# A two-layer transformer kernel in split fp32: the SBUF start addresses of the low weight halves, of the matmul operands and of the last product's operand are shifted

## The reference, cut to what matters

```
D_MODEL = 2048; SEQ = 256; DEPTH = 2; D_FF = 5632
for i in range(DEPTH):
    a = _rmsnorm(h, norm_mix[i])
    y = _mla(a, ...) if i == 0 else _swa_sinks(a, ...)
    h = h + y
    h = h + _conv_ffn(_rmsnorm(h, norm_ffn[i]), ffn_w_in[i], ffn_conv_w[i], ffn_conv_b[i], ffn_w_out[i])
return _rmsnorm(h, final_norm)
```

## Time and profile before

| | |
|---|---|
| median of 3 runs | 1988.99 us (1988.56 to 1989.11) |
| the profiled execution: its own time | 1988.18 us |
| its span, first to last instruction | 1986.3 us |
| TensorE busy | 1974.7 us, 99% of the span |
| DVE, ACT, POOL busy | 71%, 50%, 7% |
| granted TensorE clock, mean | 0.999 of full |
| moved by DMA | 379.69 MB, mean 191 GB/s |

### The profile page before, as it was taken

One profiled execution on the slowest core, in us unless ns is written; L12 is line 12 of the kernel. 1 busy time (PEld: TensorE's weight loads), 2 busy tenths in 40 slices (PEclk: granted clock), 3 DMA queues, 4 the chain that ended last, 5 costly groups with the idle time before them and its releaser, 6 DMA issues.

```text
span 1986.3 us, 33224 instructions
## 1 busy us (share of the span) xinstructions
PE 1974.7 (99%) x11726; PEld 1746.8 (88%) x11726; DVE 1418.6 (71%) x1969; ACT 991.5 (50%) x1180; POOL 143.8 (7%) x157
## 2 busy tenths in 40 slices
PE   9999999999999999999999999999999999999998
PEld 8998888888888888888899999888888888888886
DVE  6856788877887787554567668778877887765444
ACT  6556445555545554334446654555455555544443
POOL 1112220000000000110120004100000000011000
PEclk9999999999999999999999999999999999999999
DMA  8566655555555555556565435655555555576664
GB/s 300 178 195 162 195 188 190 180 194 197 183 176 191 193 197 192 190 181 201 191 229 190 136 129 173 199 191 189 172 195 194 190 188 187 197 251 214 216 193 140
DMA packets 106871, 379.69 MB, mean 191 GB/s; under 512 B 12107, under 2 KB 12684, under 8 KB 106668
## 3 DMA queue, kind: packets, MB, share of 16 engines
q1 hardware_dynamic: 102332, 362.22, 55.4%
q0 software_dynamic: 4176, 16.07, 3.2%
q10 hardware_dynamic: 288, 0.33, 0.1%
HBM read 368.09 MB, written 10.49 MB: 191 GB/s over the span
## 4 chain that ended last, share of the span: by engine, by line
PE 96%; DVE 2%; DMA 1%; ACT 0%; issue 0%; SPq 0%; ACTq 0%
PE ps L429 46%; PE ps L432 24%; PE ps L822 4%; PE ps L821 4%; PE ps L823 4%; PE ps L723 2%; PE ps L724 2%; PE ps L725 2%; DMA raw<-weights 1%; DVE w_lo L1172 1%; PE ps L761 1%; PE ps L784 1%; PE ps L459 1%; PE ps L460 1%; PE ps L458 1%; PE ps L772 1%
## 5 line engine op out<-in xcount | busy, mean ns | idle before, releaser
L1172 DVE TENSOR_TENSOR w_lo<-raw,w_hi 128x1024 fp32r<-128x1024 f32 (+1 forms) x678 | 824.8, 1230 | 493.5 <-ACT w_hi L861 472.3
L861 ACT ACTIVATE w_hi<-raw 128x1024 fp32r<-128x1024 f32 (+1 forms) x678 | 710.2, 1054 | 773.3 <-PE ps L432 455.1
L429 PE MATMUL ps<-op_in,w_hi 128*128 128x512 f32 x2992 | 1026.5, 391 | 0.4 <-DVE w_lo L1172 0.4
L432 PE MATMUL ps<-op_in,w_lo 128*128 128x256 f32 x2992 | 812.4, 282 | 0.0
L429 PEld LDWEIGHTS ps<-op_in,w_hi 128*128 128x128 f32 x2992 | 549.0, 188 | 104.5 <-issue 0.7
L432 PEld LDWEIGHTS ps<-op_in,w_lo 128*128 128x128 f32 x2992 | 565.1, 189 | 15.7
L429 PE MATMUL ps<-op_ffn,w_hi 128*128 128x512 f32 x704 | 243.1, 390 | 0.0
L432 PE MATMUL ps<-op_ffn,w_lo 128*128 128x256 f32 x704 | 195.9, 282 | 0.0
L429 PEld LDWEIGHTS ps<-op_ffn,w_hi 128*128 128x128 f32 x704 | 131.1, 188 | 26.5
L822 PE MATMUL ps<-w_lo,op_ffn 128*128 128x512 f32 x352 | 138.7, 394 | 0.0
L821 PE MATMUL ps<-w_hi,op_ffn 128*128 128x512 f32 x352 | 138.0, 392 | 0.0
(11 more groups left out here) (218 smaller groups left out, 2054.2 us busy)
## 6 DMA issues: line engine op xcount, KB each, us to landing
raw<-weights SPq DMA_DIRECT2D x662, 512.0 KB, 4.0
raw<-weights SPq DMA_DIRECT2D x16, 384.0 KB, 3.3
bias_rows<-brow POOLq DMA_DIRECT2D x1, 6144.0 KB, 36.2
win_bias<-bias_rows POOLq DMA_DIRECT2D x4, 1024.0 KB, 8.1
h<-xt SPq DMA_DIRECT2D x8, 256.0 KB, 6.7
raw<-weights SPq DMA_DIRECT2D x8, 256.0 KB, 5.7
x_tok<-x_rows SPq DMA_DIRECT2D x4, 512.0 KB, 8.9
h_rows<-h_blocks POOLq DMA_DIRECT2D x16, 128.0 KB, 5.7
```

The source lines that it names most:

```text
L429: return mm(ps[:, bank, 0:2 * T], whi, op, start=start, stop=stop)
L432: return mm(ps[:, bank, 0:T], wlo, op[:, 0, :], start=False, stop=False)
L861: f(w_hi[s][:, 0:cols], raw[s][:, 0:cols], ACT.Copy).then_inc(hi_ready, 1)
L1172: v.tensor_tensor(w_lo[s][:, 0:cols], raw[s][:, 0:cols], w_hi[s][:, 0:cols].bitcast(F32), ALU.subtract).then_inc(lo_ready, 1)
```

## The change

No instruction is added, removed or moved: the program of every engine is the same, with the same waits, and only the addresses of tiles differ. A helper `at_256(place)` moves the next free byte up to one whose remainder by 256 is `place`. It is called ahead of `w_hi`, where it moves nothing, ahead of `w_lo`, and ahead of the operands. The offset of `op_ffn[1]` against `op_ffn[0]` grows from 160 to 192 bytes, and `par` loses 256 bytes that nothing used.

```
@@ -184,7 +184,13 @@
     raw = [new(f"raw{s}", [P, CH]) for s in range(SLOTS)]
+    def at_256(place):
+
+        top[0] += (place - top[0]) % 256
+
+    at_256(128)
     w_hi = [new(f"w_hi{s}", [P, CH], F32R) for s in range(SLOTS)]
+    at_256(64)
     w_lo = [new(f"w_lo{s}", [P, CH], F32R) for s in range(SLOTS)]
     h = new("h", [P, KT, T])
...
-    par = new("par", [P, 7 * P])
+    par = new("par", [P, PC_END])
...
-    top[0] = (top[0] + 127) // 128 * 128 + 32
+    at_256(64)
     ra = region(KT * 2 * T * 4)
     op_in = place("op_in", [P, KT, 2, T], F32R, ra)
...
-    rg = region(FT * 2 * T * 4 + 160)
+    rg = region(FT * 2 * T * 4 + 192)
     r_o = rg + 57344
-    op_ffn = [place("op_ffn0", [P, FT, 2, T], F32R, rg), place("op_ffn1", [P, FT, 2, T], F32R, rg + 160)]
+    op_ffn = [place("op_ffn0", [P, FT, 2, T], F32R, rg), place("op_ffn1", [P, FT, 2, T], F32R, rg + 192)]
```

## The result

The changed kernel takes 2006.32 us in the median (2006.23 to 2006.98, 4 runs) against 1988.78 us before in the same comparison: a ratio of 1.0089, 95% interval 1.0072 to 1.0107. It is 17.5 us slower. The prediction was 1980.9 us, within 1967 to 1997.

What follows compares the result with a forecast made beforehand. TensorE's matmul periods were taken to bound the kernel. Gains of 4.1 (512 columns), 3.4 (256 columns) and 0.6 us (token triples) sum to 8.1; 1988.18 less that gives 1980.1, plus 0.8 for the median 1980.9 us, range 1967 to 1997.

Steps and rivals of the forecast that it cites:

- What bounds the kernel: Whole kernel: how fast TensorE's matmuls follow each other sets the time, neither HBM nor the splits; TensorE busy 1974.7 of 1986.3 us.
- I take the 1.0 ns as the price of the moving tile's odd start: 512-column matmuls in pairs: 230.0 ns against the last product's 229.0, the difference put down to a start off multiples of 64.
- differ in exactly that: The three groups with the most matmuls: claimed to differ in whether moving or loaded tiles start at multiples of 64.
- 512 columns in pairs: The 512-column half of each pair (512 and 256 columns together): 4144 x 1.0 ns, 4.1 us gained.
- 256 columns: Pairs and narrow triples, 5584 matmuls of 256 columns: 0.6 of the 1.0 ns each, 3.4 us gained.
- Token triples: 288 matmuls at 118.3 ns with the loaded tile at 160: 2.1 ns less each, 0.6 us gained.
- the bound "nothing": 512-column matmuls in pairs: lower bound of the gain, since mixing two lengths could cost that nanosecond as well.
- Last product at nothing: 1056 matmuls with starts at multiples of 64 before and after: costed at nothing; one nanosecond would be 1.1 us.
- The slower rival: Loads of `w_lo` from the operand's start by 256 clash with streaming: 1.5 ns a load, 6.9 us, 1996 us; chance 0.18.
- The large gain: All matmuls: the 5% surplus a column is two reads meeting, removable by good placement; 1894 us at its far end; chance 0.07.
- The argument from the Trainium skill: TensorE's array: two independent ports, so loading takes no bandwidth from the running matmul; the sum would be 0, 1989 us.
- The 8 and 13 ns over N/2.4 + 2.5: Periods of 116.8 (256 columns) and 229.0 ns (512) against 109.2 and 215.8: something costs more than the page allows.

Runs made afterwards that it cites:

- first map: Kernel without the model: uniform rows and pairs at 64 placements of streamed and loaded tile; 226.7 to 234.4 ns per 512-column matmul, pairs 349.9 ns at the changed kernel's distances.
- second map: The first map's kernel with other rows (smaller loads, 384 columns, 16-byte steps, triples, pairs); at the changed kernel's distances, last product 686.7 ns a triple, pairs 340.0 ns.

## Why the prediction was wrong

- **What bounds the kernel** was right. (The shares read with it hold for the two long stretches of the earlier trace rows only: between 1045 and 1203 us DVE is at 69% and ACT at 57%, and ACT's 42% is that of the last product. Nothing rests on this.) Periods of matmuls set the time, and three of them account for the whole difference of 18.1 us. DVE, ACT and the DMAs took no part, and the early, paced part kept its time.
- **The step that failed** is "I take the 1.0 ns as the price of the moving tile's odd start", and with it the sentence that the groups "differ in exactly that". The groups differed in distance and in sequence too, and I picked the remainder of the start by 64. Moving every matmul tile by 32 bytes changed nothing (346.8, 228.9 and 116.7 ns again), so that remainder has no price. What sets the period is the distances between loaded and streamed tiles, here (-32, -32) in pairs and -64 in the last product, together with what runs ahead of a row. Not even a distance has a price of its own: the changed kernel's (+64, 0) gave 350.0 ns and, behind another order, 340.0.
- **512 columns in pairs**: expected -4.1 us. **256 columns**, in pairs and narrow triples: expected -3.4 us. Measured: pairs, both halves together, +13.8 us, narrow triples +1.0 us. **Token triples**: expected 2.1 ns less each, measured, over the eight runs of 12 ahead of layer 1's attention, 118.1 to 118.5 ns before and 117.9 to 118.8 after. Even the bound "nothing" was on the wrong side, because I let the rows that I had seen be the ends.
- **Last product at nothing**: +3.4 us. The text said that if it moved by several nanoseconds the whole reading was wrong, and it moved by 9.7 a triple. Its distances went from -64 throughout to 128 and -64 in turn; putting it at 0 throughout saved 2.5 us, so that this term too hangs on the distances.
- **The slower rival** had the right sign and the wrong cause. It held equal starts to be the harm; distance 0 is the cheapest of all in a uniform row (226.7 ns), taking the equal starts away made pairs worse (353.3), and with `w_lo` still at the operand's start pairs reached 340 ns. In turn with -64, though, distance 0 made the last product 13.2 ns a triple dearer, so that equal starts are not always harmless either. The rival's price, 1.5 ns a load from the token triple, was no measure of this.
- **The large gain** was given 0.07. Its size, 95 us at the far end, was not found, but its core, that the surplus over the bare stream depends on placement, was nearer than the forecast: a pair can have 340.0, 346.7, 350.0 or 353.3 ns.
- The argument from the Trainium skill, "TensorE: Matmul & The Clock Gate", section "Step-by-step: what each phase is for", that loading takes no bandwidth from the running matmul, does not hold for these fp32r matmuls as a statement on time: with the loads' count and size fixed, the start of the loaded tile moves a 512-column period from 226.7 to 234.4 ns. The measurement decides. The 8 and 13 ns over N/2.4 + 2.5 were weaker evidence than the prediction made of them: it names that formula as one for an isolated matmul itself, and each one here has a load of its own.
- **What stays open**: what in the memory or in the array makes the distance count, and how what runs ahead picks a pattern. Loads of half the columns kept most of the surplus, so that it does not simply grow with the bytes of the load. That what runs ahead counts is shown by two orders, and by equal groups in one order; how it does is not explained. What the last product's new sequence would give at best was only mapped: its real value at distances 128 and -64 (696.6) is not the map's (686.7).

## What to carry to other kernels

Where TensorE is busy all the time, read the distance between starts of matmuls and compare it over placements in a small kernel that runs the program's real sequence, its group ends included; a row of equal matmuls gives the wrong ranking. Change one start at a time, and name the distance between loaded and streamed tile for every form of product, because one tile serves several. Judge such a kernel over several groups, since the first and the second of two equal ones can differ. A few rows in a trace differ in many things at once: a nanosecond between two of them is no price until one experiment has varied that thing alone.

## What the runs showed of the hardware

- A uniform row of fp32r matmuls of 512 columns takes 226.7 to 234.4 ns, by the distance of loaded and streamed start by 256 (starts in steps of 32 bytes); the absolute place has no effect beyond 1.0 ns, and 0.2 at six of the eight distances.
- In the kernels here rows of pairs settle at 340.0, 346.7, 350.0 or 353.3 ns, which at the granted 2.4 GHz are 816, 832, 840 and 848 cycles, all multiples of 8. In the first map 84 of 128 blocks of pairs have one of the last three, the others lie between 347 and 353 ns. The same distances in the same order have given 340.0 and 350.0 ns, and 340.0 and 353.3, each for a whole group.
- A small change of order in the last chunk of each group moved the pattern of nearly all the other chunks and the time of the program by 31.6 us, 1.6%.
- For 256-column matmuls the placement (+64, +64) gives 113.4 ns in most of layer 1's narrow triples, 3.3 below the kernel before, and 353.3 ns in pairs, the worst of all kernels here. The second map gave 117.8 for narrow triples at these distances, so that these hang on more than the distance too.
